# One transformer-style layer on one core: the second expert block's rows transposed in the middle of the first block, router results taken from their banks tile by tile

## What is computed

```python
def hier_moe(h, w_rg, b_rg, w_re, b_re, w_gate, w_up, w_down):      # h: 512 x 1024
    grp_prob = softmax(h @ w_rg + b_rg)                             # 4 groups
    p_grp, g_idx = top_k(grp_prob, 1)
    exp_logits = (h @ w_re + b_re).reshape(-1, 4, 4)                # 16 experts
    sel_logits = exp_logits of the chosen group
    w_top, e_loc = top_k(softmax(sel_logits), 2)
    gates = ...                                                     # two experts for each token
    for e in range(16):
        a = silu(h @ w_gate[e]) * (h @ w_up[e])                     # 1024 x 512 each
        y = y + gates[:, e:e + 1] * (a @ w_down[e])                 # 512 x 1024
```

## Time and profile before

| | us |
|---|---|
| median of 3 runs | 842.38 |
| the three runs | 845.26, 835.3, 842.38 |
| the profiled execution, whole | 835.02 |
| its span, first to last instruction | 833.2 |
| PE busy in the span | 767.9 |
| DVE busy | 605.9 |
| ACT busy | 457.6 |

### The profile page before, as it was taken

The page is one execution under the profiler, slowest core; times in us unless marked ns, Lnnn a source line. Parts: engine busy times, 40 slices in busy tenths (PEclk is TensorE's granted clock), DMA queues, the critical chain, the costliest instruction groups (busy, mean ns, idle before and its releaser), DMA issues.

```text
span 833.2 us, 10882 instructions
## 1 busy us (share of the span) xinstructions
PE 767.9 (92%) x3722; PEld 624.0 (75%) x3722; DVE 605.9 (73%) x921; ACT 457.6 (55%) x672; POOL 73.6 (9%) x86
## 2 busy tenths in 40 slices
PE   5799999988988999999895898999999999999994
PEld 3564858776877899978774587778888888888883
DVE  5468383996899578624538357879999989999882
ACT  6653233121234766622357243468888788888772
POOL 0000000000000000000000000102232223232111
PEclk8899999999999799989999799899999999999997
DMA  8720203020120200012221187599999999999941
GB/s 287 272 84 19 77 25 101 26 76 1 51 76 26 101 1 2 1 40 88 76 77 50 39 325 274 213 369 356 376 372 370 373 379 384 372 377 372 336 170 20
DMA packets 28542, 146.53 MB, mean 176 GB/s; under 512 B 4791, under 2 KB 6711, under 8 KB 21976
## 3 DMA queue, kind: packets, MB, share of 16 engines
q1 hardware_dynamic: 23320, 135.53, 43.7%
q0 software_dynamic: 5184, 10.50, 4.8%
HBM read 141.81 MB, written 12.58 MB: 185 GB/s over the span
## 4 chain that ended last, share of the span: by engine, by line
PE 75%; DVE 13%; ACT 5%; DMA 3%; issue 2%; SPq 1%; POOL 0%; DVEq 0%; POOLq 0%; ACTq 0%
PE bank L1817 16%; PE bank L1762 15%; PE bank L2141 11%; PE bank L2143 11%; PE bank L2142 10%; PE bank L1769 4%; PE bank L1829 2%; PE bank L2136 2%; DMA x_in<-in_x 1%; DMA w_raw<-in_w_in 1%; PE bank L2053 1%; DVE w_lo L1051 1%; PE bank L2055 1%; PE bank L2054 1%; ACT junk L628 1%
## 5 line engine op out<-in xcount | busy, mean ns | idle before, releaser
L1688 DVE TENSOR_TENSOR e_lo<-slot,e_hi 128x1024 fp32r<-128x1024 f32 x192 | 221.5, 1219 | 9.7 <-ACT e_hi L937 9.5
L937 ACT ACTIVATE e_hi<-slot 128x1024 fp32r<-128x1024 f32 x192 | 188.6, 1061 | 9.7 <-PE bank L2143 6.6
L1051 DVE TENSOR_TENSOR w_lo<-w_raw,w_hi 128x1024 fp32r<-128x1024 f32 x41 | 49.6, 1223 | 77.5 <-ACT w_hi L667 77.3
L2141 PE MATMUL bank<-e_hi,hgT_hi 128*128 128x512 f32 x256 | 102.0, 399 | 1.4 <-DVE hgT_lo L1706 1.2
L667 ACT ACTIVATE w_hi<-w_raw 128x1024 fp32r<-128x1024 f32 x41 | 42.8, 1062 | 108.5 <-DMA w_raw<-in_w_in 63.6
L2143 PE MATMUL bank<-e_hi,hgT_lo 128*128 128x512 f32 x256 | 100.7, 393 | 0.0
L2142 PE MATMUL bank<-e_lo,hgT_hi 128*128 128x512 f32 x256 | 100.3, 392 | 0.0
L2141 PEld LDWEIGHTS bank<-e_hi,hgT_hi 128*128 128x128 f32 x256 | 48.7, 190 | 11.6 <-DVE hgT_lo L1706 1.4
L2143 PEld LDWEIGHTS bank<-e_hi,hgT_lo 128*128 128x128 f32 x256 | 48.4, 189 | 10.4
L2142 PEld LDWEIGHTS bank<-e_lo,hgT_hi 128*128 128x128 f32 x256 | 48.6, 190 | 9.7
L2141 PE MATMUL bank<-e_hi,gaT_hi 128*128 128x512 f32 x120 | 48.1, 401 | 0.0
(11 more groups left out here) (370 smaller groups left out, 1698.1 us busy)
## 6 DMA issues: line engine op xcount, KB each, us to landing
slot<-in_w_down SPq DMA_DIRECT2D x16, 2048.0 KB, 15.9
slot<-in_w_gate SPq DMA_DIRECT2D x16, 2048.0 KB, 14.6
slot<-in_w_up SPq DMA_DIRECT2D x16, 2048.0 KB, 15.7
w_raw<-in_w_in SPq DMA_DIRECT2D x18, 512.0 KB, 3.6
w_raw<-in_w_out SPq DMA_DIRECT2D x8, 512.0 KB, 3.7
w_raw<-in_w_k_mem SPq DMA_DIRECT2D x4, 512.0 KB, 6.3
x_in<-in_x SPq DMA_DIRECT2D x4, 512.0 KB, 9.2
w_raw<-in_w_v_mem SPq DMA_DIRECT2D x4, 512.0 KB, 5.3
```

The source lines that it names most:

```text
L937: act.activation(e_hi[buffer(b, j)][:], slot[slot_][:, 1024 * part:1024 * (part + 1)], ACT.Copy).then_inc(s_ehi, 1)
L1051: dve.tensor_tensor(w_lo[slot_][:], w_raw[slot_][:], w_hi[slot_][:].bitcast(F32), ALU.subtract)\
L1688: dve.tensor_tensor(e_lo[slot_][:, at_], slot[slot_][:, at_], e_hi[buffer(b, j)][:].bitcast(F32), ALU.subtract)\
L2141: pe.matmul(dst, act_hi, w_hi_, start=first, stop=False)
```

## The change

There are two independent edits.

1. Block 1's split rows get tiles of their own, `second_hi` and `second_lo`. So PE can transpose them while block 0's parts are still read: `rows_T(1)` now stands between gate and up of block 0. ACT splits them before it takes silu of block 0, DVE before it splits block 1's gate weights. `acts_T(0)` moves from the end of turn 0 to between gate and up of block 1, and the splits of its result move behind block 1's up pieces. PE's wait on `s_mul` at the start of block 1 becomes one on `s_silu` (bank 2 has been read).
2. `tile_logits(0)` moves from behind the splits of tiles 2 and 3 to behind those of tile 1; `tile_logits(1)` moves ahead of the first split of tile 3.

```diff
+        second_hi = at("second_hi", 187, [P, KT * P], F32R)
+        second_lo = at("second_lo", 191, [P, KT * P], F32R)
...
@@ ACT, turn
-                if not isinstance(b, int) or b >= 1:
+                first, second = (isinstance(b, int) and b == n for n in range(2))
+                if not first and not second:
                     actT_hi(b - 1)
-                first = isinstance(b, int) and b == 0
-                hi_parts(b, q, 4, 8 if first else 9)
+                hi_parts(b, q, 4, 8 if first or second else 9)
+                if second:
+                    actT_hi(0)
+                    hi_parts(b, q, 8, 9)
+                if first:
+                    wait_filled(act, ("gates",))
+                    rows_hi(1, second_hi)
                 silu(b)
...
-                rows_hi(b + 1)
+                    rows_hi(b + 1)
@@ DVE, the router stage
             x2T_lo(1)
+            tile_logits(0)
             tile_residual(3, 0)
             tile_xn(2)
             x2T_lo(2)
+            tile_logits(1)
             x2T_lo(3, (0,))
-            tile_logits(0)
-            tile_logits(1)
             tile_residual(3, 1)
@@ DVE, turn
-                if isinstance(b, int) and b == 0:
+                if first:
                     lo_parts(b, q, 4, 8)
+                    rows_lo(1, second_hi, second_lo)
                     lo_parts(1, 1, 0, 4)
+                elif second:
+                    lo_parts(b, q, 4, 8)
+                    actT_lo(0)
+                    lo_parts(b, q, 8, PIECES)
                 else:
                     lo_parts(b, q, 4, PIECES)
                 act_mul(b)
-                rows_lo(b + 1)
+                if not first:
+                    rows_lo(b + 1)
@@ PE, gate_up
+                if second:
+                    pe.wait_ge(s_silu, 1)
+                elif not first:
                     pe.wait_ge(s_mul, b)
                 for j in range(8):
+                    if first and j == 4:
+                        rows_T(1, 1)
+                    if second and j == 4:
+                        acts_T(0)
@@ PE, turn
                 gate_up(b, q)
-                rows_T(b + 1, 1 - q)
                 if not isinstance(b, int) or b >= 1:
+                    rows_T(b + 1, 1 - q)
                     down(b - 1, 1 - q, b)
-                acts_T(b)
+                    acts_T(b)
```

More of the change, by code:

```diff
@@ L2145, in gate_up @@
             def gate_up(b, q):
-                if isinstance(b, int) and b == 0:
+                first, second = (isinstance(b, int) and b == n for n in range(2))
+                rows_hi_, rows_lo_ = (second_hi, second_lo) if second else (hgT_hi, hgT_lo)
+                if first:
                     pe.wait_ge(s_first_lo, 1)
```

11 lines of the change are left out of this document (5 added, 6 removed).

## The result

The changed kernel takes 829.94 us (median of 19 runs, 828.45 to 836.25), the kernel before, run beside it, 836.09 us (median of 19). The ratio is 0.9926, with a 95% interval of 0.9908 to 0.9945: **6.2 us less, 4.6 to 7.7 us by the interval**. I had forecast 4.9 us less.

The account below looks back on a forecast made before the run. The stream of weights was taken to set the end, with PE ahead by a shrinking lead. Router 2.2 us plus 2.7 of block 1's 3.9 us made 4.9 us: 842.4 - 4.9 = 837.5 us, range 828.5 to 844.

Parts of the forecast that it names:

- The router stage: Reading the first router product earlier removes PE's 2.15 us idle after three groups of transposes: 2.2 us, bounds 0 and 2.4.
- The rival that it doesn't free PE: In the router stage PE meets another wait of the same length, so only 2.7 us are left: 839.7 us; chance 0.10.
- The fillers: Eight half-clock filler products before the first block's transposes: the shift may gain 0 to 1.8 us or lose as much; taken 0.
- Block 1's rows on PE: At block 1's gate, PE saves 2.0 us dead time, 1.6 of lower clock and 0.3 for the first product: 3.9 us.
- Added on ACT and DVE: Reordered splits and an in-line table load around blocks 0 and 1 leave PE 0.3 us margin: cost 0, bounds 0 and 1.2.
- a drain beside the load: At ACT's table switch, about 1.38 us more, 2.66 in all; PE would idle 1.1 us and save 2.8.
- The stream of weights gives back only 2.7 of the 3.9 us: In the expert stage, transfers use earlier issues only where idle, 549 to 577 us; the other 1.2 us lengthen the queue.
- That PE is the bound to the end: Transfers have a little more in them, so all 6.1 us count: 836.3 us, or 834.5 with the clock's 1.8; chance 0.24.
- a limit of about 358 GB/s for a core's reads: In the expert stage, 6.3 MB a turn would take 17.6 us, about PE's own time; kin to the no-gap rival, chance 0.17.
- The clock didn't turn it around: Rival: a longer queue makes PE wait in turns 13 to 15 and lose clock, 5.9 us more: 848.3 us; chance 0.07.
- The median: Whole kernel: 842.4 us, the median of the runs shown, less 4.9 us gives 837.5 us; forecast chance 0.42.

Follow-up runs that it names:

- silu first: The changed kernel with ScalarE's table load and silu of block 0's first turn ahead of its copy of block 1's rows; ratio 0.9905 to the kernel before.

## Why the prediction was right in sign and size, and which step failed

**The router stage: right, slightly small.** Forecast 2.2 us, bounds 0 and 2.4. The wait of 2.15 us is gone wherever the edit is made. Counted from PE's first transposes, A is 40.3 to 40.4 us with the old order (four kernels) and 37.8 to 38.0 us with the new one (five), where nothing disturbs it: 2.4 to 2.5 us. What I had not priced is the clock behind this wait. In two of six profiles with the old order the products behind it fell to half clock, and there the edit is worth 4.0 us. The rival that it doesn't free PE has fallen.

**The fillers: 0 was right in the middle, and the noise lies here.** The eight fillers took 3.2 us in four of the seven profiles with the router edit that have them, and 3.59 us in the others and in all six with the old order: 0.4 us of gain at most. The 18 fillers ran slowly in some executions of kernels with either order. In those A is longer by 1.4 us with the new order and by 2.9 us with the old one, which has the slow products ahead of the fillers as well. How often either happens, and so how much of the measured 6.2 us comes from it, I can't say from one profile for each kernel.

**Block 1's rows on PE: right.** Forecast 3.9 us, measured 3.6 in seven kernels and 3.9 with silu first (229.19 - 225.33). Of the parts, the clock with the first product was right at 1.9, and the dead time then comes to 2.0, as forecast.

**Added on ACT and DVE: 0, and it was 0.2 us.** The narrow margin was right, forecast 0.3 us and read 0.2. But it is too narrow for the first weight load, and this is the 0.2 us that is missing from the 3.9. The Trainium skill, page "ScalarE: Activation LUTs", section "What ACT_TABLE_LOAD costs", has a drain beside the load; by it block 1's gate would have waited 1.1 us. In line, between a copy and silu, the load cost 1.28 us and no drain.

**The stream of weights gives back only 2.7 of the 3.9 us: wrong.** This is the step that failed. I read the growth of the landing times (7.8 to 25.5 us) as a stream that needs more time than PE and so sets the end. But a load that takes longer to land while PE never waits for it costs nothing. C is the same with three quarters of the bytes, so the pace is PE's, and the stream simply moved faster when its issues came faster (381 GB/s from 549 to 577 us). In place of the 1.2 us that I let the stream keep, it kept nothing in C. In D it kept 0.5 us as a wait in the last turn in three profiles with the block edit, and no such wait in the changed kernel's own, whose D is 0.5 us longer all the same: 0.2 us of that is the last landing (14.0 us for 13.8), and the rest lies behind PE's last product. What I had right was that the end, D, stands on the last landing. Only, that load is issued when PE lets it go, and then takes about 14 us: it is a tail of PE's work and hands on what PE gains. Its length is not quite fixed: the landing took 13.1 to 14.7 us, and the wait for it brings the 1.6 us at half clock that I had counted for the stall but not here.

**The rivals.** That PE is the bound to the end was the true case: 6.1 us by its sum, 6.2 by the stretches of the two edits apart. The measured interval alone (4.6 to 7.7 us) would have held the forecast's 4.9 too; the stretches decide. The Trainium skill has a limit of about 358 GB/s for a core's reads (page "DMA: Bandwidth & Descriptors", section "Where 436 GB/s comes from"). My prediction set 375 GB/s against it, and that was a wrong comparison, for the number counts gathers and scatters too. The queue of the weight loads alone, in the changed kernel at 600 to 700 us and at 544 to 562 us (packets, MB, share):

```profile
q1 hardware_dynamic: 2402, 34.92, 88.5%
```

```profile
q1 hardware_dynamic: 475, 7.00, 92.1%
```

These are 349 and 389 GB/s: below that limit over 100 us, above it over 18 us. So it doesn't hold for the shorter stretch, and the longer one can't decide; no run here shows the neighbouring core. The clock didn't turn it around. But it was close: with the block edit alone the last gate load landed after 27.0 us, where I let it begin from 27.1, and PE did wait 0.5 us in the last turn there.

**The median** was missed by 7.6 us: 6.3 of the level of the kernel before, 1.3 of the stream's term.

## What to carry to other kernels

A queue that grows is not yet a bound. Before letting a stream keep part of a gain, look for the first engine that waits for one of its landings; if there is none until the last turn, take the whole gain of the engine and price the tail by itself. Where runs differ by more than the effect, measure between landmarks inside the trace: here the same 3.6 us stood in seven profiles to 0.1 us, while the ratios of single edits couldn't be told from 1. Choose landmarks on the engine that is the bound: DVE's first `xn` slipped by up to 0.8 us against PE. And price a wait of that engine with the slow products that may follow it: here about 2 us of waiting brought some 1.6 us more in block 1 and at the end every time, and in the router stage in two of six profiles.

## What the runs showed of the hardware

The last transfers of a kernel can be a chain of their own. Two indirect scatters that add to the same output cost 5.9 to 6.2 us from the issue of the first to the release of the second, and this replaced the weights' landing as the end as soon as that came 2 us earlier. Of four quarter loads that were issued one behind the other the first landed after 7.0 to 9.3 us and the last after 11.1 to 14.4. At the end of the kernel, waits of TensorE of 2.0 to 2.7 us were followed by eight products at half clock in six profiles, and waits of 0.6 and 1.4 us by none in four. And eight fewer filler products on an otherwise idle TensorE saved nothing: the 20 fillers behind them went from about 4.8 to 7.54 us, mostly at half clock.
